# A hybrid decoder layer: the opening's second diagonals, one scaled block and one low part each moved one place ahead

## The reference, cut to what matters

```python
cond = jax.nn.silu(c)
mod = cond @ w_ada[layer] + b_ada[layer]          # 1024 -> 6 * 1024
shift1, scale1, gate1, shift2, scale2, gate2 = jnp.split(mod, N_MOD, axis=-1)
h = modulate(rms_norm(x), shift1, scale1)         # rms_norm(x) * (1 + scale1) + shift1
y = hybrid_mixer(h, ...)                          # h @ w_in, two groups of gated linear attention, @ w_out
x = x + gate1 * y
...                                               # the same with shift2, scale2, gate2 around a squared-ReLU MLP
return rms_norm(x, final_norm_g)
```

## Time and profile before

| what | us |
|---|---|
| median of 3 runs (lowest to highest) | 1146.87 (1145.69 to 1147.95) |
| the profiled execution's own time | 1145.04 |
| its span in the profile | 1143.3 |
| PE busy | 1125.0 (98%) |
| DVE busy | 874.7 (77%) |
| ACT busy | 612.9 (54%) |
| POOL busy | 495.3 (43%) |

### The profile page before, as it was taken

One profiled execution on the slowest core, in us unless ns is written; L12 is line 12 of the kernel. 1 busy time (PEld: TensorE's weight loads), 2 busy tenths in 40 slices (PEclk: granted clock), 3 DMA queues, 4 the chain that ended last, 5 costly groups with the idle time before them and its releaser, 6 DMA issues.

```text
span 1143.3 us, 15529 instructions
## 1 busy us (share of the span) xinstructions
PE 1125.0 (98%) x5483; PEld 933.3 (82%) x5483; DVE 874.7 (77%) x1035; ACT 612.9 (54%) x933; POOL 495.3 (43%) x318
## 2 busy tenths in 40 slices
PE   6999999999999999999999999999999999999997
PEld 6888787888888888888888888888888888888886
DVE  6998987789788776379975675567795885966776
ACT  7763554766656675256555455545664433524425
POOL 1021023245354355347542434243576675665750
PEclk9999999999999999999999999999999999999998
DMA  9777477445363467513255533554425537447203
GB/s 362 270 235 260 148 187 216 98 127 158 107 186 93 140 186 239 183 60 125 102 166 175 183 130 120 174 184 160 153 75 181 197 102 263 161 129 280 69 1 148
DMA packets 163092, 186.71 MB, mean 163 GB/s; under 512 B 7620, under 2 KB 119368, under 8 KB 160072
## 3 DMA queue, kind: packets, MB, share of 16 engines
q1 hardware_dynamic: 160616, 179.44, 47.3%
q0 software_dynamic: 2400, 6.29, 2.8%
HBM read 138.51 MB, written 40.89 MB: 157 GB/s over the span
## 4 chain that ended last, share of the span: by engine, by line
PE 93%; DVE 2%; issue 1%; ACT 1%; SPq 1%; DMA 1%; POOL 0%; DVEq 0%; ACTq 0%
PE unit_bank L1807 20%; PE unit_bank L2262 9%; PE unit_bank L2264 9%; PE unit_bank L2263 9%; PE small_bank L2262 9%; PE small_bank L2263 9%; PE small_bank L2264 9%; PE small_bank L1807 4%; PE unit_bank L2095 4%; PE unit_bank L2097 3%; PE unit_bank L2096 3%; DVE ada_acc L2363 1%; PE small_bank L1846 1%; PE small_bank L1949 1%; PE small_bank L1968 1%
## 5 line engine op out<-in xcount | busy, mean ns | idle before, releaser
L1040 POOL TENSOR_TENSOR wr_lo<-quarter,wr_hi 128x512 fp32r<-128x512 f32 x122 | 196.5, 1623 | 174.0 <-ACT wr_hi L1596 173.8
L2262 PE MATMUL unit_bank<-op_hi,wr_hi 128*128 128x512 f32 x452 | 176.6, 391 | 0.2 <-issue 0.2
L2264 PE MATMUL unit_bank<-op_hi,wr_lo 128*128 128x512 f32 x452 | 175.9, 389 | 0.0
L2263 PE MATMUL unit_bank<-op_lo,wr_hi 128*128 128x512 f32 x452 | 175.8, 389 | 0.0
L2262 PE MATMUL small_bank<-op_hi,wr_hi 128*128 128x512 f32 x448 | 174.5, 389 | 0.0
L2263 PE MATMUL small_bank<-op_lo,wr_hi 128*128 128x512 f32 x448 | 174.3, 389 | 0.0
L2264 PE MATMUL small_bank<-op_hi,wr_lo 128*128 128x512 f32 x448 | 174.3, 389 | 0.0
L1596 ACT ACTIVATE wr_hi<-wr_full 128x512 fp32r<-128x512 f32 x90 | 56.8, 631 | 176.4 <-DVE wr_full L3045 172.0
L3045 DVE TENSOR_TENSOR wr_full<-quarter,quarter 128x512 f32<-128x512 f32 x90 | 89.1, 991 | 56.7 <-PE small_bank L2264 22.9
L1596 ACT ACTIVATE wr_hi<-quarter 128x512 fp32r<-128x512 f32 x136 | 82.8, 625 | 86.9 <-PE unit_bank L2264 48.6
L1807 PE MATMUL unit_bank<-a_hi,w_hi 128*128 128x512 f32 x304 | 121.0, 398 | 0.0
(11 more groups left out here) (387 smaller groups left out, 2371.3 us busy)
## 6 DMA issues: line engine op xcount, KB each, us to landing
quarter<-in_w_mlp_dram SPq DMA_DIRECT2D x128, 256.0 KB, 4.3
hidden_scratch<-hid SPq DMA_DIRECT2D x98, 256.0 KB, 2.4
ada_slot<-in_w_ada_dram SPq DMA_DIRECT2D x48, 512.0 KB, 6.6
op_full<-hidden_scratch SPq DMA_DIRECT2D x21, 1024.0 KB, 4.9
pair_quarter<-in_w_in_dram SPq DMA_DIRECT2D x32, 256.0 KB, 3.2
piece_x<-t_scratch SPq DMA_DIRECT2D x16, 512.0 KB, 4.7
piece_y<-t_scratch SPq DMA_DIRECT2D x32, 256.0 KB, 3.4
raw<-in_w_out_dram SPq DMA_DIRECT2D x16, 512.0 KB, 4.8
```

Source lines behind the costliest of these rows:

```text
L1040: pool.tensor_tensor(wr_lo[slot][:, :, :], split_source(n), wr_hi[slot][:, :, :].bitcast(F32), ALU.subtract).then_inc(wr_lo_pool, 1)
L2262: pe.matmul(dst, wh, ah, start=opens, stop=False, skip_group_check=True)
L2263: pe.matmul(dst, wh, al, start=False, stop=False, skip_group_check=True)
L2264: mm = pe.matmul(dst, wl, ah, start=False, stop=k == KH - 1, skip_group_check=True)
```

## The change

Four moves, no instruction added or taken away:

- ACT copies block 11 before it waits for the first two `finish_ada`; before, this copy stood behind the first high part.
- PE makes block 11 before the first two `first_ada`; before, behind them.
- DVE makes the second diagonals before `add_ada(0)`; before, behind it.
- DVE makes `low_input(4)` before `add_ada(15)`; before, behind it.

```diff
@@ ACT
-            for n in range(11):
+            for n in range(12):
                 if n in (4, 7):
                     copy_x(TT - 2 if n == 4 else TT - 1)
                 copy_scaled(n)
@@ ACT
-                    for n in ({1: (11, 12), 2: (13,), 4: (14, 15)}, {})[half].get(k, ()):
+                    for n in ({1: (12,), 2: (13,), 4: (14, 15)}, {})[half].get(k, ()):
                         copy_scaled(n)
@@ PE
-                if n == 11:
+                if n == 12:
                     pe.wait_ge(read["rows"], 1)
                     for q in range(2):
                         first_ada(q, 2 + q)
@@ DVE
             low_weights_first(1)
+            diagonals(1)
             for n in range(16):
+                if n == 15:
+                    low_input(4)
                 add_ada(n)
-                if n == 0:
-                    diagonals(1)
                 if n == 9:
                     finish_ada(0, 0, 2)
                     finish_ada(0, 1, 3)
-                if n >= 11:
+                if 11 <= n < 15:
                     low_input(n - 11)
```

## The result

The changed kernel is slower: median 1148.88 us (1146.49 to 1152.77, 22 runs) against 1146.95 us (1145.41 to 1149.02, 22 runs) for the kernel before, a ratio of 1.0018 with a 95% interval of 1.0012 to 1.0024, so +2.1 us (0.0018 x 1147). It lies inside the range given and just under the bound of 0.2%, but at two and a half times the +0.8 us of the forecast's own case.

A forecast was written before the change was run, and what follows sets the result against it. PE, busy 1125.0 of 1143.3 us, bounds the kernel, and DVE's list sets its opening. Terms -0.09, +0.36, +0.60, less 0.09, give +0.8 us: 1146.87 to 1147.7 us, range 1145.8 to 1149.8.

The forecast's parts named there:

- the forecast's own case: Whole kernel: +0.8 us, to 1147.7 us against the median, with a chance of 0.55.
- DVE's list sets the opening: In the opening, the chain of sums on DVE, not PE, decides when the opening ends.
- add_ada(0) at 0.75 us: DVE, behind the moved diagonals: add_ada(0) was to take 0.75 us instead of 1.30, starting after POOL's instruction ends.
- The price: DVE's first sum: its 1.30 us, against 0.75 later, was read as the price of POOL's instruction running beside it.
- the hand-over of 0.1 us: Between dependent sums on DVE: the next starts 0.1 us behind the end of the one before, taken from the trace.
- DVE's list by -0.09 us: DVE's chain of sums: add_ada(1) was to start at 20.45 instead of 20.54, moving the list by -0.09 us.
- The low part ahead of the last sum, +0.78 us: DVE, before add_ada(15): low part waits for ACT and delays the last sum; PE's second finishing products start +0.78 us later.
- The slack of 0.09 us: Between the last sum's end and PE's second finishing products: 0.09 us beside the hand-over, subtracted from the delay.
- The clock rival: Opening: PE's clock falls behind either pair of finishing products; +1.2 us at the first, +2.5 at the second; chance 0.15.
- The clock of 0.50 behind 30 us: Sign of a wrong forecast: PE's granted clock at 0.50 (1.2 GHz) anywhere behind 30 us.
- The sum's +0.8 us: DVE's steps in series: shift -0.09, new wait +0.36, low part's own +0.60, less slack 0.09: +0.78, or 0.8 us.
- PE's first input product near 36.6: PE, opening: ACT's earlier copies let the first input product start at 36.59 instead of 37.21, without reaching the end.

The follow-up runs named there:

- both filled: Changed kernel with products filling PE's waits ahead of both pairs of finishing products, five 128x128 and four 128x512: ratio 1.0003 against the kernel before.
- fill ahead: Changed kernel with four extra 128x512 products filling PE's wait ahead of its second finishing products: ratio 1.0006 against the kernel before.
- sums later: Changed kernel with PE's second finishing products moved behind the second half's first input tile: ratio 1.0004 against the kernel before.
- the pair with the fill ahead and behind: Changed kernel with four extra 128x512 products ahead of PE's second finishing products, or behind them: ratios 1.0006 and 1.0034 against the kernel before.

## Why the prediction was right, and where it was off

- **DVE's list sets the opening: right.** Diagonals alone and block 11 alone change nothing that can be told.
- **add_ada(0) at 0.75 us: right, and for the reason given.** It took 0.74 in all eight profiles with the diagonals ahead of it, against 1.10 to 1.30 in the five in which it stands first. No run was made for the cause, but the thirteen profiles show it: whichever DVE instruction lies beside POOL's (L979) ends 0.54 to 0.56 us behind POOL's end, wherever it started. Before, add_ada(0) ends at 19.81 and POOL's at 19.26; in the changed kernel the diagonals end at 20.32 and POOL's at 19.78. The price didn't go away, it went over to the diagonals and got smaller: they take 0.74 to 0.85 us in the eight, 0.69 in the five. The prediction had them at 0.69. Its 0.85 us from add_ada(0) to the next sum is met, 0.85 to 0.87, so the hand-over of 0.1 us that it kept in the sum is there.
- **DVE's list by -0.09 us: not to be seen.** add_ada(1) starts anywhere from 20.14 to 21.68 in the eight profiles and from 20.04 to 21.31 in the five, mostly by when the root comes. From the root's end to it are 1.79 us in the kernel before and 1.85 in the changed kernel's first profile, the diagonals' price beside POOL's instruction included.
- **The low part ahead of the last sum, +0.78 us: the right place, the wait right, the size a little low.** 0.32 us of DVE waiting for ACT (0.36 forecast), 0.88 and 0.68 us of PE waiting (0.9 forecast). Taking it back removed the loss. With the clock held up at the second pair, the runs put it at 0.03 to 0.06% (both filled, fill ahead), 0.3 to 0.7 us with intervals of 1 us on either side. The traces are finer: from add_ada(1) to the first `w2s` product it is 37.29 us in the kernel before and 37.30 in the first profile of block 11 only, 38.28 and 38.23 in the two kernels with the low part ahead and that wait filled, so 1.0 us, as the 1.02 above. The slack of 0.09 us that the sum took off was not there: the hand-over from a sum to single-column products takes 0.14 to 0.15 us wherever PE waits for it, not the 0.06 taken from a turn, and the kernel before has the same 0.15 (42.22 to 42.37).
- **The chances: the step that failed.** The clock rival had 0.15, and it is half of the loss or more: 0.16 to 0.18% with it, 0.03 to 0.06% with the waits filled. I priced it rightly (1.7 us for a stretch of 3.4 us behind the second pair, seen there twice, and twice as long once; up to 0.4 us at the first pair was too little, 1.02 measured), named both places, and then held the shortness of each idle stretch against it. The clock of 0.50 behind 30 us, which I had named as a sign of being wrong, is in both profiles of the changed kernel. Of four profiles with the unfilled wait three show the fall behind the second pair, of the nine profiles of the eight other kernels none. The mean granted clock of all runs points the same way beyond the profiles: 0.9946 over the 11 runs of the changed kernel against 0.9957 over the 29 of the kernel before beside them, but 0.9963, 0.9967 and 0.9970 with the second wait filled, against 0.9959 to 0.9961 beside those. It counts falls that DVE hides too, so it gives no size: diagonals only, whose time is that of before, has 0.9949 over ten of its eleven runs (the eleventh has 0.945 at an ordinary time).
- **The sum's +0.8 us against 2.1 measured** is mostly that term left at nothing. The direction comes from the low part, rightly. The range holds because the rival stood in it, and that the result still counts as "same", at 0.18% against a bound of 0.2%, is luck.
- **PE's first input product near 36.6** came at 37.30 (later root) and 38.75 (blocks 12 to 15 at half rate). Neither reached the end: in the first profile tile 3 still waits for DVE, as forecast, and in the second PE still waits 0.68 us for the last sum behind it.

## What to carry to other kernels

Moving work ahead of an instruction that TensorE waits for can cost more than the wait: here, where single-column products followed, the clock fell behind it, so count the clock behind the wait too. An independent product in the gap, useful if there is one and useless if not, can pay for itself; and before an early result is made at the price of a late one, ask which of the two the next engine wants first. One profile tells one state of the clock, so whether an engine arrives just in time has to be read from more than one.

## What the runs showed of the hardware that I had not expected

A fall of the clock came behind idle times far shorter than the 2.03 us of the kernel before, when the 16 single-column products followed them: 0.86, 0.88 and 1.31 us ahead of the second pair (falls at 46.4, 44.8 and 46.6). Filling the wait took these away; the same products behind it did not. Falls around 33 us follow the first pair too, behind 0.50 us at the shortest (block 11 only), but for those another reading is open, as said above. Behind the products with no idle time ahead of them no profile has a fall, and idle time ahead of other work mostly went by: 0.83 us ahead of the first input product in four profiles, and 0.90 to 1.90 us ahead of the turn before block 4 in eight, while 1.96 and 2.03 us there have one behind them. That it takes both is read from these rows; no run put other work than the single columns behind the same wait. It isn't certain even with both: 1.12 and 0.98 us and the first pair (the changed kernel's first profile, and sums later), and 0.68 us and the second pair in its second profile, went by without a fall. The Trainium skill (TensorE: Matmul & The Clock Gate, section "Why this matters for your kernels") warns of idle gaps between bursts alone, and of much longer ones than these; by that warning none of these stretches would have mattered, and the pair with the fill ahead and behind decides against it. The same page (section "What's actually happening") says that the point of a change of clock isn't tied to the kernel's start and varies from run to run. The profiles agree: one and the same kernel fell at 44.8 us in one execution and at 30.8 in another. That may be why its runs spread over 6.3 us where the kernel before spreads over 3.6, and those with both waits filled over 2.1; with so few profiles this is not shown.
